# Hybrid decoder step with a two-level mixture of experts, one core: the next rows' gather cut in four and placed between the pairs of gate and up chunks

## The reference

```
h    = LN0(x) * (1 + scale1) + shift1;  [q|k|v|u] = h @ w_in
o    = [rms(window_attention) * g | rms(S5 scan, gelu, GLU) * g] @ w_out
x    = LN1(alpha * x + gate1 * o)
h2   = LN0(x) * (1 + scale2) + shift2
comb = top-1 of 4 expert groups, then top-2 of its 8 experts      # 576 (row, expert) pairs
f    = sum over e of comb[:, e] * ((silu(h2 @ w_gate[e]) * (h2 @ w_up[e])) @ w_down[e])
x    = LN2(alpha * x + gate2 * f) * ln2_g + ln2_b
```

## Time and profile before

| | us |
|---|---|
| median of 3 runs | 1650.84 (1650.09 to 1652.15) |
| the profiled execution | 1649.67 |
| its span, first to last instruction | 1647.8 |
| outside the span | 1.9 |
| PE busy in the span | 1521.8 (92%), 8533 matmul records |
| DVE busy | 505.2 (31%) |
| ACT busy | 245.2 (15%) |
| POOL busy | 142.0 (9%) |
| moved by DMA | 559.69 MB |
| blocks of experts | 31, the first begins at 691 us, the last ends at 1595 us |

### The profile page before, as it was taken

The page is one execution under the profiler, slowest core; times in us unless marked ns, Lnnn a source line. Parts: engine busy times, 40 slices in busy tenths (PEclk is TensorE's granted clock), DMA queues, the critical chain, the costliest instruction groups (busy, mean ns, idle before and its releaser), DMA issues.

```text
span 1647.8 us, 22763 instructions
## 1 busy us (share of the span) xinstructions
PE 1521.8 (92%) x8533; PEld 656.2 (40%) x8534; DVE 505.2 (31%) x1428; ACT 245.2 (15%) x531; POOL 142.0 (9%) x215
## 2 busy tenths in 40 slices
PE   3899999999999899999999999999999999999974
PEld 2457555456344444433333333333333333333321
DVE  6467345222233265731212121121111211211216
ACT  2220000042213322111111110100100100100111
POOL 6001000131210230010000000000000000000010
PEclk9999999999699899899999999999999999999997
DMA  9995788873186879988996999999999999999943
GB/s 293 386 387 182 282 301 292 291 219 103 55 302 251 317 267 395 397 336 337 422 422 279 423 421 421 421 422 421 421 422 421 421 421 422 422 421 422 422 169 157
DMA packets 119287, 559.69 MB, mean 340 GB/s; under 512 B 15657, under 2 KB 20553, under 8 KB 64921
## 3 DMA queue, kind: packets, MB, share of 16 engines
q1 hardware_dynamic: 100800, 510.20, 77.8%
q0 software_dynamic: 17952, 46.05, 8.2%
q10 hardware_dynamic: 482, 2.70, 0.6%
HBM read 565.78 MB, written 42.37 MB: 369 GB/s over the span
## 4 chain that ended last, share of the span: by engine, by line
PE 60%; DMA 35%; DVE 3%; issue 1%; ACT 1%; POOL 0%; SPq 0%; POOLq 0%; DVEq 0%; ACTq 0%
DMA ring<-in_exp_w_up 31%; PE bank L752 14%; PE bank L2336 6%; PE bank L2244 5%; PE bank L770 5%; PE bank L2093 4%; PE bank L346 3%; PE bank L726 3%; DMA ring<-in_w_in 2%; PE bank L2287 2%; PE bank L2176 2%; DMA ring<-in_ada_w 2%; PE bank L739 1%; PE bank L836 1%; PE bank L2071 1%
## 5 line engine op out<-in xcount | busy, mean ns | idle before, releaser
L752 PE MATMUL bank<-ring,BC 128*64 128x512 f32 x1984 | 455.4, 594 | 36.2 <-DMA ring<-in_exp_w_up 35.2
L752 PEld LDWEIGHTS bank<-ring,BC 128*64 128x64 f32 x1984 | 147.2, 137 | 338.5 <-issue 267.7
L770 PE MATMUL bank<-ring,BC 128*64 128x512 f32 x992 | 219.7, 595 | 0.0
L614 DVE TENSOR_TENSOR BC<-BC,bank 64x512 f32<-64x512 f32 x31 | 21.4, 691 | 463.1 <-ACT BC L692 463.1
L726 PE MATMUL bank<-H,MOD 128*64 128x512 f32 x512 | 131.6, 592 | 0.3 <-DVE H L1950 0.3
L770 PEld LDWEIGHTS bank<-ring,BC 128*64 128x64 f32 x992 | 68.5, 137 | 127.7 <-issue 123.9
L550 POOL DMA_INDIRECT y_dram<-BC,y_row x31 | 29.9, 966 | 857.6 <-DVE y_row L624 741.6
L2336 PE MATMUL bank<-ring,MT 128*128 128x512 f32 x224 | 101.8, 608 | 1.0 <-issue 0.8
L2244 PE MATMUL bank<-ring,MT 128*128 128x512 f32 x192 | 85.4, 598 | 1.0 <-ACT X L1166 1.0
L692 ACT ACTIVATE BC<-bank 64x512 f32<-64x512 f32 x31 | 18.2, 588 | 451.5 <-PE bank L752 451.5
L2093 PE MATMUL bank<-MT,ring 128*128 128x288 f32 x256 | 66.2, 422 | 6.3 <-DMA ring<-in_w_in 4.0
(11 more groups left out here) (543 smaller groups left out, 1459.1 us busy)
## 6 DMA issues: line engine op xcount, KB each, us to landing
ring<-in_exp_w_gate SPq DMA_DIRECT2D x128, 1024.0 KB
ring<-in_exp_w_up SPq DMA_DIRECT2D x128, 1024.0 KB
ring<-in_exp_w_down SPq DMA_DIRECT2D x128, 1024.0 KB
ring<-in_ada_w SPq DMA_DIRECT2D x96, 1024.0 KB
ring<-in_w_in SPq DMA_DIRECT2D x20, 1024.0 KB
y_dram<-con POOLq DMA_DIRECT2D x20, 1024.0 KB, 34.1
ring<-in_w_out SPq DMA_DIRECT2D x16, 1024.0 KB
ring<-in_ssm_glu_w SPq DMA_DIRECT2D x4, 1024.0 KB
```

The lines of the kernel that those rows point to most:

```text
L752: mm = pe.matmul(bank[64 * i:64 * i + 64, 2, :], xT[:, q // 2, k % 4, 64 * (q % 2):64 * (q % 2) + 64], ring[:, at, 512 * (k % 4):512 * (k ...
L770: mm = pe.matmul(bank[64 * (c % 2):64 * (c % 2) + 64, 4 + c // 2, :], aT[:, j, :], ring[:, at, 512 * c:512 * c + 512], start=(j == 0), sto ...
```

## The change

Four things:
- The gather of the next block's rows moves from behind the gate and up matmuls to between them: both prompt blocks of the first half of the width in front of pair 0, one prompt block of the second half in front of pair 1, the other in front of pair 2, and the sample rows in front of pair 3. The block therefore waits for `sel_ready` at its start.
- `turn(e + 1)` moves from behind the transposes of the activation to ahead of them, directly behind the last gate and up matmul. On ACT and DVE `rows_out` moves ahead of silu and of the multiplication.
- The fetch of the last norm's rows moves from ahead of POOL's loop to behind its final gathers; DVE waits for it just ahead of its first use instead of at the head of the tail.
- `sel` moves by 62 columns within the same tile.

```diff
-        sel = MODf[:, 1218:1410].rearrange("p (b s) -> p b s", b=3)
+        sel = MODf[:, 1280:1472].rearrange("p (b s) -> p b s", b=3)
...
 def moe_pool(pool):
-            pool.wait_ge(S("x1_ready"), 2)
-            pool.dma_start(GE[:, 0, :], a["ln2_g"].to_broadcast([P, D])).then_inc(S("ln2_in"), 16)
...
 def moe_dve(...), body(e):
+                rows_out(e + 1)
                 dve.wait_ge(S("sg_ready"), e + 1)
                 V.tensor_tensor(AC[hi, :], SG[hi, :], bank[hi, 2, :], ALU.mult).then_inc(S("act_ready"), 1)
-                rows_out(e + 1)
                 turned_out(e + 1)
...
 def moe_act(act), body(e):
+                rows_out(e + 1)
                 act.wait_ge(used, len(plan) + e * RING + 8)
                 nc.scalar.activation(SG[hi, :], bank[0:64, 2, :], ACT.Silu).then_inc(S("sg_ready"), 1)
-                rows_out(e + 1)
...
 def moe_pe(pe):
+            def gather_rows(i, b):
+                for h in range(2):
+                    q = 2 * i + h
+                    pe.matmul(bank[64 * h:64 * h + 64, i, :], sel[:, b, :], H[:, b, 512 * q:512 * q + 512],
+                              start=(b == 0), stop=False)
+            def gather_samples():
                 for q in range(4):
...
             def body(e):
                 place = pe.value_load(...)
                 pe.wait_ge(S("xg_ready"), 2 * e + 2)
+                pe.wait_ge(S("sel_ready"), e + 2)
                 for k in range(KD):
+                    if k == 0:
+                        gather_rows(0, 0)
+                        gather_rows(0, 1)
+                    elif k == 4:
+                        gather_rows(1, 0)
+                    elif k == 8:
+                        gather_rows(1, 1)
+                    elif k == 12:
+                        gather_samples()
                     for i in range(2):
...
-                gather(e + 1)
+                turn(e + 1)
                 pe.wait_ge(S("rint_ready"), since("rint_ready") + 4)
                 pe.wait_ge(S("act_ready"), e + 1)
                 for j in range(4):
                     mm = pe.transpose(bank[:, 3, SLOTS * j:SLOTS * j + SLOTS], AC[hi, j:FE:4], ident[hi, 64:128])
                 mm.then_inc(S("at_ps"), 1)
-                turn(e + 1)
...
 def tail_pool(pool):
+            pool.wait_ge(S("x1_ready"), 2)
+            pool.dma_start(GE[:, 0, :], a["ln2_g"].to_broadcast([P, D])).then_inc(S("ln2_in"), 16)
...
 def tail_dve(dve):
             dve.wait_ge(S("g2_ready"), 5)
-            dve.wait_ge(S("ln2_in"), 160)
             add(1, Yq[0], 7, G2s, xq, mq[:, 16:17])
...
             go(V.reciprocal(mq[:, 28:29], mq[:, 27:28]))
+            dve.wait_ge(S("ln2_in"), 160)
             go(V.scalar_tensor_tensor(out=xq, in0=xq, scalar=mq[:, 24:25], in1=g2_q, op0=ALU.subtract, op1=ALU.mult))
```

More of the change, by code:

```diff
@@ L716, in moe_pe, with gather_first @@
         def moe_pe(pe):
-            def gather(it, finished=False):
+            def gather_first(it):
                 pe.wait_ge(S("sel_ready"), it + 1)
-                for i in ((1, 0) if finished else (0, 1)):
-                    if finished:
-                        pe.wait_ge(S("h2_ready"), 8 - 4 * i)
+                for i in (1, 0):
+                    pe.wait_ge(S("h2_ready"), 8 - 4 * i)
                     for b in range(2):
[L724 to L727, removed]
+                        gather_rows(i, b)
+                gather_samples()
[5 more added lines that the diff above has]
+            def gather_samples():
                 for q in range(4):
@@ L772, in body @@
                     mm.then_inc(used, 1)
-            gather(0, True)
+            gather_first(0)
             pe.wait_ge(S("xf_ready"), since("xf_ready") + 1)
@@ L800, in tail_pool @@
                         .then_inc(S(f"y_in{b}"), 16)
+            pool.wait_ge(S("x1_ready"), 2)
+            pool.dma_start(GE[:, 0, :], a["ln2_g"].to_broadcast([P, D])).then_inc(S("ln2_in"), 16)
+            pool.dma_start(GE[:, 1, :], a["ln2_b"].to_broadcast([P, D])).then_inc(S("ln2_in"), 16)
+            for x, t in (("ln2_g", g2_q), ("ln2_b", b2_q)):
+                for q in range(4):
+                    pool.dma_start(t[32 * q:32 * q + 32, :], a[x][:, 512 * q:512 * q + 512].to_broadcast([32, 512]))\
+                        .then_inc(S("ln2_in"), 16)
         def tail_sp(sp):
```

## The result

The changed kernel takes 1659.99 us, the median of 18 runs (1651.28 to 1662.09), against 1651.21 (1644.29 to 1653.27, 18 runs) for the kernel before: a ratio of 1.0053 with a 95% interval of 1.0043 to 1.0062, some 8.8 us slower (7.1 to 10.2 by that interval). Its profiled execution took 1657.65, 8.0 more than the one shown before. Forecast were +4.7 us, 1655.5, in a range from 1649.3 to 1660.0: the measured median lies 0.01 us inside the upper end.

A forecast was written before the change was run, and what follows sets the result against it. Bound: PE until DMA restarts behind the second hole, then the DMA stream, then PE work behind the last landings. +1.61 + 5.18 + 1.72 - 3.80 = +4.7 us, median 1655.5, range 1649.3 to 1660.0.

The forecast's parts named there:

- Block 0 waits for select(1): At the head of block 0, PE waits for sel_ready and everything on PE behind it shifts by +1.61 us.
- A block while PE is the bound: Hand-overs around gather and down cost +0.74 us a block, +5.18 over seven blocks ahead of the DMA restart (2.1 to 9.1).
- Pair 0 released later: Eight gather records stand in front of pair 0's 16 records, so its release comes +1.72 us later in the block.
- The switch of form: On PE, a switch is seen as 0.52 against 0.2145; the skill's drain reading would add +2.2 us over seven blocks.
- The last block: Down starts 2.63 instead of 6.43 us behind the last gate and up record: -3.80 us (0 to -3.9).
- The stream behind the hole: Where DMA is the bound, no byte less is streamed: 0 per block, bound 2 us over some 20 blocks.
- The rows of the last norm: Moving their 2.6 MB fetch to the tail gains nobody anything: 0, upper bound +2.3 us.
- rival D: In the tail, POOL gets no further while DVE is busy, so the fetch comes late: some 12 us more, 1667; chance 0.03.
- Rival A: Second half bound by the PE, slot, DMA round, not DMA: 18 x 2.43 = 44 us less, 1611; chance 0.07.
- Rival B: The last norm's 2.6 MB did lengthen the stream: -6.2 us, in all -1.5, 1649.3; chance 0.08.
- Rival C: In the first loop, ACT's table load comes to lie behind gate and up: 9.0 us more, 1664.5; chance 0.07.
- E: Nothing measurable, first-half terms at their lower ends: +1.6 us, 1652.4; the forecast's near end, no separate chance.

The follow-up runs named there:

- e8: Kernel before with the changed order in the second loop only, last norm's rows fetched at their old place; ratio 0.9978 to the kernel before.
- e9: Changed kernel with the order of before in the second loop, changed order in the first, fetch moved; ratio 1.0072 to the kernel before.
- e4: Changed kernel with the whole gather, samples too, ahead of pair 0; ratio 1.0066 to the kernel before, median 1659.2 us.
- e6: Changed kernel with select(1) ahead of turned_out(0) on DVE; ratio 1.0037 to the kernel before, median 1657.3 us.
- e5: Changed kernel with the sample rows gathered behind the last pair, then activation transposes and turn, silu and multiplication ahead of the copies; ratio 1.0047 to the kernel before.
- e3: Changed kernel with every piece of the gather one pair later and the wait for sel_ready ahead of pair 1; ratio 1.0050 to the kernel before.
- e0: The changed kernel once more, nothing altered; ratio 1.0057 to the kernel before.
- e7: Kernel before with the changed order in the second loop only and the last norm's fetch moved; ratio 0.9988 to the kernel before.
- e1: Kernel before with only the fetch of the last norm's rows moved behind the final gathers; ratio 1.0001 to the kernel before.
- e10: The same kernel as e1, run a second time; ratio 1.0005 to the kernel before.
- e2: Changed kernel with turn put back behind the activation's transposes; ratio 1.0180 to the kernel before.
- e11: The kernel before itself, run again for a second profile; ratio 0.9996.

## Why the prediction was right, and where its sizes were off

- *What bounds the kernel.* Right. The end is the restart of DMA behind the second hole, a stream whose length the PE order hardly touches, and the last block. e8 and e9 show the two ends of it apart, and the first column passes into the last down one for one in e4, e6 and e9, whose second columns are within 0.2 those of the changed kernel or of the kernel before.
- *Block 0 waits for select(1): +1.61, bounds 0 and 1.8.* The start moved by 1.61 (693.16 less 691.02 and less the 0.53 of the earlier stages). But the term was too small, 3.3 in all and outside its bounds: PE came back from the wait at half clock and the first gather took 1.7 us more. The prediction counted the wait and not what the wait does to the clock, although it had both levels of it in the profile of before. e6 shows it: 1.34 of standing, clock kept, 2.75 us back. This is the one term that was missing.
- *A block while PE is the bound: +0.74.* Measured 0.90. Down started 2.74 behind the last gate and up record, not 2.63, and the samples in the middle took 1.16, not 1.11. Over seven blocks 6.3 instead of 5.2. The two stalls, 0.35 and 0.5, came out at 0.37 and 0.54. e5 agrees with this account: without the samples inside gate and up 1.16 less, with down 0.57 later, 0.59 in sum; its period is 0.57 shorter, 27.58.
- *Pair 0 released later: +1.72.* Measured 1.71, and e3 and e4 moved it both ways as worked out.
- *The switch of form.* By the Trainium skill ("TensorEngine Tiling (Array Packing)", Key Properties) each of the switches drains the array, which had given +2.2 over seven blocks on top. The measured period lies midway, 0.16 a block above the reading from the rows and 0.15 below the drain's, so it decides between neither. The 0.31 that the prediction took for a switch was misread, though: the records start two by two, one such pair every 0.43, so a start 0.52 behind the last is a step only 0.10 longer. The earlier trace rows have it too: the 16 gather records need 3.43 and the samples start 3.53 behind their first (977.27 to 980.80). In the changed kernel the samples cost 0.10 ahead, 1.02 themselves and 0.05 behind; that the prediction's 1.11 came out so near is luck: its 0.31 ahead and its 0.2 given back are both misread and nearly cancel.
- *The last block: -3.80.* Measured -3.46. Pair 3's up records run 0.33 behind its gate records (the first at 1590.41 against 1590.08, where in the blocks of the first half the two start within 0.01), as if its up chunk landed that much later, so the pair takes 3.98 instead of 3.64; the rest is as worked out to 0.1. The down chunks were there.
- *The stream behind the hole: 0 with 2 us of room.* Right for the changed kernel, and for e0, e4, e6 and e8 (699.1 to 699.3). Not right everywhere: see below.
- *The rows of the last norm: 0.* Right in time for the change as it stands. The DMA engines finished with them near 1632, 7 us ahead of the first use. Of rival D, beside which stood a rule of the Trainium skill ("SBUF — State Buffer", the "DVE blocks DMA" trap): POOL's four issues took 2.05 us, 0.51 each, while a DVE operation from SBUF to SBUF ran beside them at 1619.31. That is the pace of the earlier trace rows; no blocking is seen here. But the Trainium skill tells this trap of DVE operations in a 2-port mode and names an fp32 tensor_copy within SBUF; the operation here was a SCALAR_TENSOR_TENSOR, so the rule itself is not tested.
- *The sum.* 1.6 + 1.7 + 6.3 + 1.7 - 3.46 = 7.8, and the last down is 7.8 later (936.8 against 929.0 from the first chunk). That lies in the interval of the medians, 7.1 to 10.2; the remaining 1 us up to 8.8 is within the tail's scatter and is not assigned.
- *The range.* The mechanism and the sign were right. That the median fell into the range was luck: it lies 0.01 us below the upper end, and that end came from giving seven blocks 1.3 each, where they took 0.90; the half clock that took up the room had no term and no bound.
- *Rival A* (the round of slots and not DMA is the limit) is out by e7, e8 and e9. *Rival B* (6 us less) is out by e1 and e10. *Rival C* is out: the table load runs behind the copy of the rows and is over before gate and up end (in block 0 from 710.42 to 711.70, and silu starts at 713.41). *E*, the near end of the forecast, did not come.

## What to carry to other kernels

When a DMA-bound stream follows a stretch in which DMA waited for buffers, only two places of the compute order counted in this kernel: what lies ahead of the last moment at which DMA ran dry, and what lies behind the last landing. Order the work for PE's period ahead of the first and for a short tail behind the second; where the loops are separate anyway, give each its own order (e8). A wait that is put at the head of an engine's stretch should be costed twice, once for its length and once for the clock that TensorE has when it comes back.

## What was not expected of the hardware

- A stall of 1.53 us on PE was followed by half clock in most blocks of e2 (down up to 8.79 instead of 7.09 us), and so was one of 2.46 us; stalls of 0.37 and 0.54, and one of 1.34 ahead of block 0 in e6, were not. In the second half of the kernel before, PE stands for 1.9 us a block at full clock, in two stalls of some 0.6 and 1.3, none longer than 1.42. In e2 itself 7 of the 31 blocks have the same stall and a down pass of 7.09. So length alone does not tell.
- A change that moves 2.6 MB out of the stretch ahead of both holes, without moving an issue of SP, made the stream behind the second hole 1.0 to 1.3 us longer (703.7 against 702.7 twice each, 700.5 against 699.2). With the changed order in the first loop it did not (699.2, and 702.9 in e9). e3 and e5 carry 1.6 and 0.7 us of the same kind. The traces narrow it down. Counted in packets, the first 12 MB behind the second hole have come 32.4 to 32.7 us after the first issue in the eight profiles without the extra (before, e11, changed, e0, e6, e4, e8, e9), and after 33.0 to 33.7 in the five with it: half of it or more arises at the restart, not in the pace of the stream. In four of the five (e1, e10, e7, e3) POOL's scatter of the block before starts 1.46 us ahead of the restart, where it is 1.95 in the kernel before. Its packets end 1.8 us behind SP's first issue instead of 1.1, and SP's own first packet starts at 1.5 to 1.6 instead of 1.0. The kernel before, then e1, each with the half us ahead of the restart (columns as in the earlier trace rows):

```profile
883.77 0.96 POOL L550 DMA_INDIRECT y_dram<-BC,y_row  x1 [26.28 <-DVE y_row L624]
885.22:885.72 0.50, 0.50 (x6) 0.20 (x4) 0.00 (x0) 0.00 (x0) 0.00 (x0) 1.00 0.89 360
```

```profile
883.16 0.96 POOL L542 DMA_INDIRECT y_dram<-BC,y_row  x1 [26.77 <-issue]
884.12:884.62 0.50, 0.50 (x6) 0.20 (x4) 0.00 (x0) 0.00 (x0) 0.00 (x0) 1.00 0.00 0
```

That this is what delays the weights is argued, not shown: e5 has its 0.7 at the restart with a scatter that is over by then. Why POOL is later, and what adds the rest, stays open; the profile does not tell the 16 engines apart, and no run here was made for it.
